# A transformer block on one core: the first chunk of tokens and the value weights issued from ScalarE's own DMA queue

## The reference

```python
mod_x = jnp.split((jax.nn.silu(c) @ w_ada[l] + b_ada[l])[:, None, :], 6, axis=-1)
mod_c = jnp.split((jax.nn.silu(c_ctx) @ w_ada[l] + b_ada[l])[None, None, :], 6, axis=-1)
...
h = modulate(x, norm_g[l, 0], mod_x[0], mod_x[1])        # rms_norm(x, g) * (1 + scale) + shift
qa, ka, va, u, qw, kw, vw, gate = split_mixer_inputs(h @ w_in[l])
...
x = x + mod_x[2] * rms_norm(mix, norm_g[l, 1])
h2 = modulate(x, norm_g[l, 2], mod_x[3], mod_x[4])
x = x + mod_x[5] * rms_norm(swiglu(h2, w_ffn_in[l], w_ffn_out[l]), norm_g[l, 3])
```

## Time and profile before

| | |
|---|---|
| median of three runs | 1982.87 us (1979.5 to 1984.51) |
| the profiled execution: time, span | 1977.57 us, 1975.5 us |
| mean granted TensorE clock | 0.968 of full speed |
| TensorE matmul | busy 1818.9 us, 92% of the span |
| VectorE, GpSimd, ScalarE | 1110.9 us (56%), 829.2 us (42%), 763.1 us (39%) |
| moved by DMA | 235.18 MB, mean 119 GB/s |

### The profile page before, as it was taken

How to read it: one execution, slowest core, us unless ns; L and a number is a source line. 1 busy time by engine, 2 the same in 40 slices (tenths; PEclk the granted TensorE clock), 3 DMA queues, 4 the chain that set the end, 5 groups by cost and what they waited for, 6 DMA issues and landing times. The chain is left out here.

```text
span 1975.5 us, 26948 instructions
## 1 busy us (share of the span) xinstructions
PE 1818.9 (92%) x9312; PEld 1534.5 (78%) x9312; DVE 1110.9 (56%) x1559; ACT 763.1 (39%) x1434; POOL 829.2 (42%) x516
## 2 busy tenths in 40 slices
PE   6897999999979989697999989789999999899998
PEld 4896888887758768496988868668888888688886
DVE  2336588778838878375763345485545444322322
ACT  2424333434327667453540025543333333232332
POOL 0124667776416994200001212375555555233433
PEclk9898999999989999898989999899999999999999
DMA  7233323435575555203012342112122221354552
GB/s 271 85 104 108 129 107 146 152 128 213 192 191 145 131 142 153 91 2 77 0 65 96 144 174 86 69 70 96 64 96 76 83 96 64 114 195 143 197 175 90
DMA packets 84201, 235.18 MB, mean 119 GB/s; under 512 B 11025, under 2 KB 24721, under 8 KB 83986
## 3 DMA queue, kind: packets, MB, share of 16 engines
q1 hardware_dynamic: 84114, 234.09, 35.9%
HBM read 180.19 MB, written 53.87 MB: 118 GB/s over the span
## 5 line engine op out<-in xcount | busy, mean ns | idle before, releaser
L677 POOL TENSOR_TENSOR ring<-raw_w,ring 128x512 fp32r<-128x512 f32 x120 | 181.1, 1521 | 162.9 <-ACT ring L566 162.7
L78 PE MATMUL psum<-h_hi,ring 128*128 128x512 f32 x400 | 156.3, 391 | 8.4 <-ACT z L612 4.2
L79 PE MATMUL psum<-h_lo,ring 128*128 128x512 f32 x400 | 155.7, 389 | 0.0
L80 PE MATMUL psum<-h_hi,ring 128*128 128x512 f32 x400 | 155.6, 389 | 0.0
L2473 DVE TENSOR_TENSOR u_lo<-stage,u_hi 128x1024 fp32r<-128x1024 f32 x44 | 58.5, 1331 | 160.7 <-ACT u_hi L2433 160.7
L78 PE MATMUL psum<-u_hi,uf_hi 128*128 128x512 f32 x352 | 138.2, 393 | 9.7 <-POOL uf_lo L2456 9.4
L2456 POOL TENSOR_TENSOR uf_lo<-u_f,uf_hi 128x512 fp32r<-128x512 f32 x44 | 78.2, 1778 | 158.9 <-ACT uf_hi L2435 158.6
L79 PE MATMUL psum<-u_lo,uf_hi 128*128 128x512 f32 x352 | 137.9, 392 | 0.0
L80 PE MATMUL psum<-u_hi,uf_lo 128*128 128x512 f32 x352 | 137.9, 392 | 0.0
L566 ACT ACTIVATE ring<-raw_w 128x512 fp32r<-128x512 f32 x120 | 73.7, 626 | 136.1 <-DVE raw_w L802 58.1
L1224 DVE TENSOR_REDUCE mx<-psum 128x1 f32<-128x1280 f32 x64 | 95.2, 1487 | 24.4 <-PE psum L1121 22.2
(11 more groups left out here) (323 smaller groups left out, 5098.4 us busy)
## 6 DMA issues: line engine op xcount, KB each, us to landing
stage<-in_w_ffn_out SPq DMA_DIRECT2D x44, 512.0 KB, 3.6
raw_w<-in_w_pairs SPq DMA_DIRECT2D x40, 512.0 KB, 4.6
qk_dram<-room SPq DMA_DIRECT2D x26, 512.0 KB, 3.6
room<-in_w_ada SPq DMA_DIRECT2D x24, 512.0 KB, 5.6
gates_dram<-ost SPq DMA_DIRECT2D x24, 512.0 KB, 3.0
b_g<-gates_dram SPq DMA_DIRECT2D x8, 1536.0 KB, 7.9
stage<-in_w_ff SPq DMA_DIRECT2D x22, 512.0 KB, 4.8
i_raw<-in_w_ff SPq DMA_DIRECT2D x22, 512.0 KB, 4.7
```

What stands on the lines that cost most here:

```text
L78: pe.matmul(out, sh, mh, start=first, stop=False, skip_group_check=onto)
L79: pe.matmul(out, sh, ml, start=False, stop=False, skip_group_check=onto)
L80: return pe.matmul(out, sl, mh, start=False, stop=last, skip_group_check=onto)
L677: pool.tensor_tensor(w_lo[i], source(p, i), w_hi[i].bitcast(F32), ALU.subtract).then_inc(w_lo_ready, 1)
```

## The change

The transfers of the first chunk of tokens and of the value weights leave SyncE's stream and stand at the head of ScalarE's, ahead of its first wait. Their destinations, sources and semaphores are the same. On SyncE's queue the pieces of `w_ada` follow directly behind the six small pieces, and the wait for the last used piece follows directly behind the sixteenth piece.

```diff
@@ mixer_in, the block of SyncE @@
             xv = io["x"].rearrange("(t p) d -> p t d", p=P)
             cv = io["ctx"].rearrange("(t p) d -> p t d", p=P)
-            sp.dma_start(xt[0][:], xv[:, 0:4, :]).then_inc(x_in[0], 16)
             for i in range(ADA):
                 if i >= ADA_BUFS:
                     sp.wait_ge(ada_used, i - ADA_BUFS + 1)
                 sp.dma_start(ada[i % ADA_BUFS], io["w_ada"][i // 2 + KC * (i % 2)]).then_inc(ada_in[i % ADA_BUFS], 16)
-            for j in range(4):
-                sp.dma_start(v_raw[:, 2 * j:2 * j + 2, :], io["w_v"][:, 2 * j:2 * j + 2, :]).then_inc(wv_in[j], 16)
             sp.wait_ge(ada_used, ADA)
             sp.dma_start(xt[1][:], xv[:, 4:8, :]).then_inc(x_in[1], 16)
@@ mixer_in, the block of ScalarE @@
+            act.dma_start(xt[0][:], io["x"].rearrange("(t p) d -> p t d", p=P)[:, 0:4, :]).then_inc(x_in[0], 16)
+            for j in range(4):
+                act.dma_start(v_raw[:, 2 * j:2 * j + 2, :], io["w_v"][:, 2 * j:2 * j + 2, :]).then_inc(wv_in[j], 16)
             act.wait_ge(small_in, 96)
             act.activation(econd[:], cond[:], ACT.Exp, scale=-1.0).then_inc(e_ready, 1)
```

## The result

The changed kernel takes 1986.05 us (median of 20 runs, 1979.59 to 1990.89) against 1981.72 us (20 runs, 1979.04 to 1985.53): ratio 1.0022, interval 1.0012 to 1.0031. It is 2.4 to 6.1 us slower. I had forecast 1980.1 us and a range up to 1985.5 us; the time lies above it, and the sign was wrong. That the step is under the 0.3% to which I gave the most chance says nothing for the reasoning: a gain was forecast, and a loss of 4.3 us came.

A forecast was written before the change was run, and what follows sets the result against it. Matmuls bound the kernel from 130 us; in the first 22 us the token chunk ends last. Tokens -2.8 us, the rest 0: 1980.1 us against the median 1982.87, range 1976.5 to 1985.5 us.

The forecast's parts named there:

- What bounds the kernel: Matmuls set the pace from 130 us on; gains or losses arise in the first 22 us and move everything behind.
- The tokens: First on ScalarE's stream, issued at 0.76 us, landing at 9.8 us instead of 12.66, range 7.7 to 12.2 us.
- The table load: On ScalarE, 1.28 us, placed directly ahead of the exponential, behind the five issues, and hidden before 7.19 us.
- The small pieces: On SyncE's queue, last landing at 8.2 us instead of 7.19, upper end 11.7 us; ScalarE free for squares at 9.9 us.
- First pieces of w_ada: On SyncE's queue, landing near 10.9 us instead of 14.06; TensorE's first group still ends before the transposes, winning nothing.
- Value weights: Four issues leave SyncE; earlier landing wins nothing, competition with w_ada might cost TensorE 0 to 1.5 us; taken as nothing.
- (c): Small pieces starve behind ScalarE's queue, delaying silu and squares: +0.7 to +2.6 us, middle 1984.5 us; chance 0.12.
- S: Landing of the last small piece; ScalarE's squares start no sooner than S + 1.68 us.
- (a): TensorE pauses over 2.7 us before the transposes, the clock falls; net -0.8 us, 1982.1 us; chance 0.18.
- (b): Tokens land no sooner because bandwidth is divided; only 0.43 us of issue time saved, 1982.4 us; chance 0.10.
- (d): A change of over 5.9 us by a mechanism not seen, clock falls shifting place; chance 0.10.
- The chances: Forecast 0.50, rivals (a) 0.18, (b) 0.10, (c) 0.12, (d) 0.10; faster 0.06, same 0.89, slower 0.05.

The follow-up runs named there:

- the split alone: Kernel before the change, conditioning vector on its own semaphore, lambda exponentials after the squares, no transfer moved: ratio 1.0014, run again 1.0001.
- the one-queue kernel: Kernel before, all transfers on SyncE, tokens second after the conditioning vector, which has its own semaphore; lambda exponentials after the squares: 1978.5 us, ratio 0.9986.
- the best with two: Kernel before with only tokens moved to ScalarE's queue, conditioning vector on its own semaphore, lambda exponentials after the squares: 1977.68 against 1980.71 us, ratio 0.9985.
- The split waits: Changed kernel, conditioning vector on its own semaphore awaited by the first exponential, lambda exponentials after the squares: 1984.54 against 1980.71 us, ratio 1.0014.
- tokens alone: Kernel before with only the first chunk of tokens moved to ScalarE's queue, value weights left on SyncE: 1981.73 against 1982.14 us, ratio 1.0007.
- The value weights alone: Kernel before with only the value weights moved to ScalarE's queue, tokens left on SyncE behind the small pieces: 1985.98 us, ratio 1.0021.
- three squares more: Kernel before with three added squares of the first token tile ahead of its statistics, nothing moved: 1989.9 against 1982.14 us, ratio 1.0041.
- issues behind the wait: Changed kernel with ScalarE's five transfer issues placed behind its wait for the small pieces: one run, 1992.2 us.

## Why the prediction was wrong, point by point

- **What bounds the kernel.** Right. A shift of the first 22 us comes out at the end in the seven kernels of the table other than the split alone, of both signs, as far as intervals of 2 to 3 us to either side can tell.
- **The tokens.** Right in direction, and more came than the forecast asked for: landed at 8.96 us, forecast 9.8 us, inside 7.7 to 12.2 us. The 0.9 us from the last byte to the semaphore had no row behind it. The table load stood behind the issues, as argued, and was hidden.
- **The small pieces: the step that failed.** I took 8.2 us "since the pieces are issued 0.47 us apart and each needs only a part of the engines' time". It was 15.15 us, beyond even the upper end of 11.7 us, and with it the squares' wait for the small pieces, not the tokens, ended last. The packet for packet price in that bound was the right mechanism; two of its terms were off. It let the alternation begin at 1.6 us, where the second queue, after its first piece, moved nothing until 5 us. And it priced the partner at 0.157 us, a packet of 4 KB, where the value weights bring larger ones. With the measured numbers: 144 of the 864 packets passed before the gap, so 45 for each engine remained. From 5 to 12 us 36 of them passed at 0.196 us, and the last 9, beside the larger packets of the value weights, some 2.5 us more, to about 14.5 us; with 0.6 us to land that is 15.1 us. The 2.5 us are read from the DMA views and not worked out, and why nothing moved before 5 us stays open.
- **The page and the trace.** The Trainium skill ("DMA: Bandwidth & Descriptors", Queues, rings and completion order) has the engines take turns by packets of several descriptors, by which I reasoned that a small piece costs one turn. What the trace lists shows one for one, 572 to 606, with rows of 4 B to 1 KB on one side and 4 to 5 KB on the other. For this case the trace decides. The other rule of the Trainium skill's page (Rules for kernel authors), that a second issuing engine only saves issue time, came out too mild in the changed kernel and fits the one-queue kernel, which is as fast as the best with two.
- **First pieces of w_ada.** Wrong by the same cause: I had the first land at 10.9 us, and it landed at 18.12 us, since it stands behind the small pieces in their queue. The split waits showed it to be worth 1.84 us by itself. Its terms as I wrote them (7.2, 2.5 and 0.9 us) give 10.6 us; in tokens alone, where the small pieces were less late, it landed at 11.99 us.
- **Value weights.** "I take nothing" was wrong, though not where I looked. I had checked only whether w_ada would starve behind TensorE's second group, which it did not. Their cost is on the small pieces: without them these land at 10.57 us, with them at 15.15 us, and the value products start at +0.83 us instead of +4.06 us. With the waits split it is the same: the first piece of w_ada lands at 12.05 us without them on ScalarE's queue and at 18.23 us with them, and the transposes start at 18.29 and 23.75 us.
- **Rivals.** (c) is what happened, and its decision point, S at 10.98 us, agrees with both runs that bear on it: at 10.57 us the tokens alone gained 0.5 us at the transposes, at 15.15 us the changed kernel lost 4.07 us. (The value weights alone lost by late tokens, not by this wait.) Its price of +0.7 to +2.6 us was too small; the last small piece came out at 15.15 us where (c) ended at 13.6 us, and 15.15 + 1.59 - 12.66 is the 4.08 us. (a) is real, seen in tokens alone (0.88 us in the group) and three squares more (2.33 us), not in the profiled execution of the changed kernel, whose pause of 2.58 us left the pace high. The length of the pause alone does not decide it here, as the two executions of the split alone show; and by my forecast of 19.1 us a pause over 2.7 us would have begun at 16.4 us, not at 15.8 us. (b) and (d) were not needed.
- **The chances.** I gave (c) 0.12 while its condition was the only one for which the profile had a number, 54 packets at a packet's time, and I put the forecast a microsecond from the lower bound with no row to rest it on. The broadcast piece's 4.1 us on a nearly empty queue should have warned me.

## What to carry to other kernels

Ask of a transfer that is moved to a second queue not only when it lands but what is in flight beside it: in this kernel the small pieces of many packets, which gate an engine, waited one large packet for each of theirs, and everything behind them in their queue waited too. Count packets for each DMA engine, not bytes. Before a queue is added, look at the order in the one there is and at waits for more than the next instruction needs: here a semaphore of its own for one small vector and the tokens moved up to second place win about 3 us on one queue, and keeping all early issues off the second queue costs nothing that these runs can tell.

## What the runs showed of the hardware that was not expected

- Two loaded queues share by packets almost exactly one for one (606 to 572 between 5 and 12 us), in both assignments of small and large, and with large ones on both sides (430 to 423 between 12 and 20 us, issues behind the wait). Bytes do not count: 211 packets with 0.00 MB passed beside 210 with 0.99 MB.
- A queue beside a loaded one can stand still for some 3 us: no small packet between 3 and 5 us in the changed kernel and in tokens alone, and no packet of the tokens between their issue at 7.62 us and 11 us in the kernel with the issues behind the wait. With only the value weights on the other queue 190 small packets moved between 3 and 5 us. Why is not settled by these runs.
- Some issues take longer: `ident` 0.59 us and `sub_g` 0.61 us in the changed kernel instead of 0.43 us each, a small part of the delay. That both engines issue at once is not the cause: in tokens alone `ident` took 0.62 us from 2.13 us on, when ScalarE's one issue had ended at 1.22 us.
- In the split alone TensorE kept the pace of its second 32 matmuls in one execution (3.65 us, after a pause of 2.73 us) and not in the other (4.84 us at a granted clock of 0.51, after 2.06 us). So the length of the pause does not tell. The changed kernel, with a pause of 2.58 us there, also spread more, over 11.3 us in 20 runs against 6.5 us; that the one causes the other was not tested.
